# RWKV triangular inverse: the chunk of 16 rows moves between the two chunks of 128 rows at each level

## The reference, cut to what matters

```
def step(S, inp):
    r_t, w_t, k_t, v_t, a_t, b_t = inp
    sa = einsum("bhij,bhj->bhi", S, a_t)
    S = S * w_t + sa[..., None] * b_t + v_t[..., None] * k_t
    y = einsum("bhij,bhj->bhi", S, r_t)
    return S, y
```

## Time and profile before

| | |
|---|---|
| device time, median of 3 runs | 2067.47 us (2066.7 to 2070.39) |
| the profiled execution | 2068.04 us, span 2066.3 us |
| PE matmul busy | 1995.1 us (97% of the span) |
| DVE busy | 1068.9 us (52%) |
| ACT busy | 923.0 us (45%) |
| POOL busy | 1282.7 us (62%) |
| the inverse's levels | about 350 to 525 us of the span |

### The profile page before, as it was taken

How to read it: one execution, slowest core, us unless ns; L and a number is a source line. 1 busy time by engine, 2 the same in 40 slices (tenths; PEclk the granted TensorE clock), 3 DMA queues, 4 the chain that set the end, 5 groups by cost and what they waited for, 6 DMA issues and landing times.

```text
span 2066.3 us, 44052 instructions
## 1 busy us (share of the span) xinstructions
PE 1995.1 (97%) x17530; PEld 1883.3 (91%) x17530; DVE 1068.9 (52%) x1648; ACT 923.0 (45%) x1618; POOL 1282.7 (62%) x528
## 2 busy tenths in 40 slices
PE   8999998999999999999998999999999989999998
PEld 8999787788799999999985999999999878899998
DVE  5781677666678726870465777020363254334431
ACT  4433553111343344333546534444446555556552
POOL 6888362000378887888630788977756554677885
PEclk9999999999999999999999999999999999999999
DMA  7455332000145444455320454544454332344552
GB/s 286 162 181 186 120 107 81 3 2 3 65 161 183 164 183 164 164 181 184 143 82 1 156 191 183 194 173 164 144 205 160 125 123 103 125 181 150 187 193 82
DMA packets 40937, 291.46 MB, mean 141 GB/s; under 512 B 4448, under 2 KB 5728, under 8 KB 5856
## 3 DMA queue, kind: packets, MB, share of 16 engines
q1 hardware_dynamic: 40512, 288.26, 39.0%
q10 hardware_dynamic: 288, 1.18, 0.2%
HBM read 288.38 MB, written 1.05 MB: 140 GB/s over the span
## 4 chain that ended last, share of the span: by engine, by line
PE 32%; issue 27%; POOLq 20%; POOL 19%; ACT 1%; DVE 1%; DVEq 0%; DMA 0%; ACTq 0%
POOLq L2093 19%; POOL w_low L2089 19%; PE ps L633 9%; PE ps L641 9%; PE ps L637 9%; PE ps L1456 2%; PE ps L1444 1%; PE ps L1434 1%; PE ps L822 0%; POOLq L2088 0%; ACT units L1995 0%; ACT units L1526 0%; POOLq L2105 0%; DMA con<-consts 0%; DVE units L2115 0%
## 5 line engine op out<-in xcount | busy, mean ns | idle before, releaser
L2089 POOL TENSOR_TENSOR w_low<-wring,w_high 128x1024 fp32r<-128x1024 f32 x524 | 1282.5, 2463 | 764.5 <-ACT w_high L1526 734.3
L633 PE MATMUL ps<-in_high,w_high 128*128 128x256 f32 (+1 forms) x2808 | 811.1, 289 | 11.6 <-POOL w_low L2089 6.4
L641 PE MATMUL ps<-in_high,w_low 128*128 128x256 f32 (+1 forms) x2808 | 802.3, 286 | 0.0
L637 PE MATMUL ps<-in_low,w_high 128*128 128x256 f32 (+1 forms) x2808 | 800.5, 285 | 0.0
L1526 ACT ACTIVATE w_high<-wring 128x1024 fp32r<-128x1024 f32 x524 | 542.6, 1056 | 259.4 <-PE ps L633 254.3
L633 PEld LDWEIGHTS ps<-in_high,w_high 128*128 128x128 f32 x2808 | 532.1, 189 | 25.5 <-issue 15.5
L641 PEld LDWEIGHTS ps<-in_high,w_low 128*128 128x128 f32 x2808 | 532.1, 189 | 0.0
L637 PEld LDWEIGHTS ps<-in_low,w_high 128*128 128x128 f32 x2808 | 531.2, 189 | 0.4
L633 PE MATMUL ps<-hid_high,w_high 128*128 128x272 f32 (+1 forms) x880 | 250.6, 285 | 0.0
L641 PE MATMUL ps<-hid_high,w_low 128*128 128x272 f32 (+1 forms) x880 | 250.5, 285 | 0.0
L637 PE MATMUL ps<-hid_low,w_high 128*128 128x272 f32 (+1 forms) x880 | 250.0, 284 | 0.0
(11 more groups left out here) (353 smaller groups left out, 2622.6 us busy)
## 6 DMA issues: line engine op xcount, KB each, us to landing
wring<-stream SPq DMA_DIRECT2D x270, 1024.0 KB, 4.8
con<-consts SPq DMA_DIRECT2D x1, 2199.0 KB, 16.2
X<-x_in SPq DMA_DIRECT2D x1, 1088.0 KB, 7.7
units<-decay ACTq DMA_DIRECT2D x1, 1024.0 KB, 4.9
out<-AL SPq DMA_DIRECT2D x1, 1024.0 KB, 4.7
AL<-stream SPq DMA_DIRECT2D x2, 256.0 KB, 20.7
par<-params SPq DMA_DIRECT2D x1, 187.0 KB, 5.5
con<-consts ACTq DMA_DIRECT2D x1, 130.0 KB, 4.8
```

The lines of the kernel that those rows point to most:

```text
L633: mm = pe.matmul(o, wh, high(k), start=(k == 0), stop=False)
L637: mm = pe.matmul(o, wh, low(k), start=False, stop=False)
L641: mm = pe.matmul(o, wl, high(k), start=False, stop=(k == kt - 1))
L2089: pool.tensor_tensor(w_low[:, (half + h) % SPLIT_RING, :], wring[:, slot, h * HALF * P:(h + 1) * HALF * P], w_high[:, (half + h) % SPLIT_R ...
```

## The change

At each level the chunk of 16 rows goes between the two of 128 rows, in U, M, masks, adds and in ACT's copies at level 0. The ticks of the work beside the levels are the same. At level 0 of group 0 the fill ahead of U2 is no longer issued, since U0 has by then written its product into bank 4; the fills ahead of U1 and U0 stay.

```diff
-        RK_ORDER = (1, 2, 0)
+        RK_ORDER = (1, 0, 2)
...
                 for n in range(LEVELS):
                     chunks = [c for c in RK_ORDER if n < RK_LEVELS[c]]
                     for c in chunks:
-                        if g == n == 0:
+                        if g == n == 0 and c < 2:
                             fill(4, 4)
```

## The result

The changed kernel took 2078.6 us (median of 12 runs, 2073.0 to 2093.56); the kernel before took 2071.3 us in the 12 runs of the same comparison (2066.7 to 2073.99). The ratio is 1.0048, 95% interval 1.0034 to 1.0062: slower by 0.48%, where 0.26% was forecast; the two medians differ by 7.3 us, 0.35%, and two later comparisons gave 0.44% and 0.30%. The kernel before was itself 3.8 us above the median of the three runs that the prediction started from. The profiled execution has a span of 2077.0 us against 2066.3, 10.7 more.

The account below looks back on a forecast made before the run. The prediction took PE's instruction stream to bound the stage; losses of 1.79 (group 0), 1.19 each (groups 1 and 2) and 1.16 (group 3) summed to 5.33 us, giving 2072.8 us on the 2067.47 median, range 2068.5 to 2076.

Parts of the forecast that it names:

- The order's price: Sum of the losses over groups 0 to 3 from what stands ahead of PE's waits: 5.33 us.
- level 3 in groups 1 and 2: Chunk 1's second score waits for DVE's mask with M0 instead of M2 as cover: loss 0.75 us per group.
- level 2: Output(1), groups 1 to 3: M0 replaces M2 under the wait, 0.59 lost, 0.15 regained at right(2); net 0.44 us each.
- group 3: Loses 0.44 us at level 2's output(1) plus 0.72 at solve(1) and solve(2): 1.16 us.
- solve(1): Group 3: waits for DVE's copy of z, now queued behind the longer add2 instead of add0; loss 0.40 us.
- solve(2): Group 3: U0 instead of U2 stands ahead of its wait, and U2 comes behind; loss 0.32 us.
- group 0: Loses 0.50 us at the start, level 1, and 1.29 at level 3's second score and turn: 1.79 us.
- Rival 1: Waits even out as a later M2 shortens later waits, such as level 5's second score; no change, chance 0.20.
- the even spread over the levels: Rival in the experiments' forecasts: any swap costs; level 3 alone 0.9, 0.6, 0.6, 0.6 us in groups 0 to 3.
- The fill: Group 0's start: dropping it frees 1.09 us of PE, costed at nothing because M1(1) waits for mask1 anyway.
- the term for the clock: Half-rate clock at group 0's start, 352 to 361 us: 3.5 us at most, left out of the sum.
- rival 2: Clock falls to half where PE idles in group 0, 352 to 361 us: 2075 to 2076.5 us, chance 0.10.

Follow-up runs that it names:

- after_again: The changed kernel run again, unchanged; ratio to the kernel before 1.0044 (1.0029 to 1.0059).
- only_level3: The kernel before with the new order at level 3 alone, on PE and DVE, all fills kept; ratio 1.0027 (1.0013 to 1.0042).
- warm_all_after: The changed kernel plus unread matmuls in its waits, at starts of groups 1 to 3 and in the gate stretch; ratio 1.0016 (1.0005 to 1.0028).
- better: Kernel before, chunk 1's second score a tick later, unread matmuls in waits and gate stretch, 26 instead of 20 ahead of rk_o; ratio 0.9976.
- three parts: The kernel before with the new order at level 3, level 2, or levels 0 and 1 (third fill gone) alone; ratios 1.0027, 1.0019, 1.0001.
- ticks_moved: The changed kernel with chunk 1's second score and output(1) one tick later on PE; ratio 1.0001 (0.9986 to 1.0016), repeated 1.0004.

## Why the prediction was off

**The order's price was right.** Forecast 5.33 us; 5.45 in parts at full clock, some 5.2 in runs at equal clock. Term by term: level 3 in groups 1 and 2, 0.75 forecast and 0.79 measured; level 2, 0.44 and 0.31; group 3, 1.16 and 1.23 (its solve(1) 0.40 and 0.52, its solve(2) 0.32 and 0.42, which leaves 0.29 for level 2); group 0, 1.79 and 1.86. The reason given is shown from both sides: new order with two ticks moved, no loss; old order with the ticks moved the other way, more loss than the change (0.67% against 0.30 to 0.48%). Rival 1, that the waits even out, is wrong: the wait of 0.43 us in level 5 that could have shrunk stayed; and the even spread over the levels is wrong too.

**The fill was worth nothing,** as costed: taken away alone it lengthens a wait from 1.02 to 2.05, put back it shortens one from 1.44 to 0.35.

**What failed is the term for the clock,** which I left out of the sum and priced in rival 2 at a chance of 0.10, in one place (352 to 361 us) and with 3.5 us at most. It measures 3.6 us in the mean, in groups 0 to 2 and the gate stretch, and falls came in every trace of the changed kernel. My argument was that the clock stood at 1.00 all through the stage although PE was busy only 3.82 of 6 us in group 0. That was one execution. In the second of the same kernel it fell at both edges of the stage, at 345 and 526 us. A single trace with the clock at 1.00 shows that it can hold, not that it does. Rival 2 had the size: it added up to 3.5 us to the order's loss, and its 2075 to 2076.5, put on the baseline of all 107 runs, becomes 2077.1 to 2078.6, where 2078.26 is the mean measured. Its chance and its place were wrong.

**The cause of the falls was named only in part.** Rival 2, like the Trainium skill's rule (TensorE: Matmul & The Clock Gate, HAM oscillation), has PE idle first: PE that idles between groups of matmuls starts the next one at half rate. The case of that section is PE waiting for DMA. The falls at 411 and 472 us agree with it, behind waits for DVE of 1.07 and 1.70 us. The one at 396 us in after_again does not: PE was busy 2.00 of 2 us ahead of it. The mean clock of the runs agrees in part: 0.9835 with the longer waits, 0.9858 with the new order and the waits gone, 0.982 with the longest waits in the old order; but only_level3, with a wait of 1.70 us ahead of the second score in three groups, has 0.9856.

**The baseline too:** of the 5.8 us between the forecast 2072.8 and the median of 2078.6, 3.8 are the kernel before, which took 2067.47 us in the three runs I started from and 2071.3 beside the changed one. Over 107 runs its mean is 2069.55, 2.1 above. On that mean my sum gives 2074.9, 3.4 us short of the changed kernel's mean.

**What stays open.** The two kernels with the most added PE work in waits and gate stretch have the highest mean clocks (warm_all_after, better), but which of their matmuls do it is not shown. Why the whole change lowers the mean clock by 0.0023 and its three parts by 0.0002 together is open too. And why a given wait or start lets the clock fall in one execution and not in the next is not shown: in ticks_moved, with the shortest waits, it fell in three groups of one trace.

## What to carry to other kernels

When streams are interleaved by ticks, an exchange of two blocks is not neutral even if the cyclic order is the same: look at what stands ahead of each wait of the work beside it, and price the exchange as the difference of the covers. Where the clock can fall, price a wait on PE twice: its length, and what follows at half rate; and count a run of small matmuls as a place where it can fall, even with PE busy throughout. Take the spread and the mean clock of many runs before trusting a trace whose clock never falls; comparing at equal mean clock, or part by part where the clock is full, separates a schedule's own cost from the clock's.

## What the runs showed of the hardware

The mean granted clock of one program differs between executions from 0.982 to 0.989 (107 runs of the kernel before), and the time with it by 8 us of 2070; a straight line in the clock takes up 80% of the variance. A fall at the start of the gate stretch came in 10 of the 17 traces of the table, and cost some 4.5 us in nine of them. The clock fell behind waits of 1.07 to 1.70 us, and also where PE had been busy 2.00 of 2 us with matmuls of 64x64 and 16x16. A kernel with matmuls whose results nobody reads, and one tick moved, was 0.24% faster than the kernel before; about 1.0 of its 4.6 us is the tick. With the matmuls alone the ratio was 0.9992 (0.9977 to 1.0007), not clear of no change.
